# A hybrid decoder layer on one core: another order of the down products, and other instruction orders at four places

## The chip, the cores and the metric

The kernel runs as one program on one core of a Trainium2 chip. The metric is the device time of the whole program in microseconds, as the median of several runs; lower is better. Before the change three runs took 2069.5, 2070.79 and 2072.06 us.

The engines are written as in the profile: PE (TensorE) multiplies, DVE (VectorE), ACT (ScalarE) and POOL (GpSimd) work on elements, SP (SyncE) issues DMAs. Each works off its own list of instructions in order; they meet only through semaphores.

## The reference

One decoder layer on x of 1024 tokens by 1024 features, in float32:

```
h = RMSNorm(x)
[q,k,v,g | x_rnn,gate_rnn | m_ret,m_rnn] = h @ W_in             # 1024 x 10240
y_ret = (silu(g) * HeadNorm(Retention(rot(q), rot(k), v))) @ W_ret_o    # 4 heads, chunks of 128
y_rnn = (RG_LRU(CausalDWConv4(x_rnn)) * gelu(gate_rnn)) @ W_rnn_o
x = x + (sigmoid(m_ret) * y_ret + sigmoid(m_rnn) * y_rnn) @ W_out
up = CausalDWConv3(RMSNorm(x) @ W_up)                           # 1024 x 5632
x = x + (silu(up[:, :2816]) * up[:, 2816:]) @ W_down            # 2816 x 1024
out = RMSNorm(x)
```

## The kernel before, in words

Every product of two float32 matrices is made of three matmuls (`mm3`, lines 308 to 310): each operand is split into a high part (ACT rounds it to fp32r, "hi") and a rest (DVE subtracts, "lo"), and hi hi, hi lo and lo hi are added in PSUM. So in front of nearly every matmul stand one ACT and one DVE instruction.

Three sections use Winograd's form of Strassen's scheme, in which seven products of half-size blocks replace eight. The input projection (28 blocks of 256 columns) and the FFN's up projection (22 blocks) have the weights W split as B11 to B22, of which DVE makes T1 to T4 (`combine_t13`, `combine_t2`, `combine_t4`), and the activations as A11 to A22, S1 to S4. A block runs the products q = 0 to 6: B11 A11 (P1), B21 A12, T4 A22, T2 S2, T1 S1, T3 S3, B22 S4, twelve matmuls of 128x512 each. Some accumulate on an earlier result: ACT first copies P1, U1, P5, U2 out of PSUM (`in_copy`, `copy_u`, lines 1313 and 1593), and the products q = 3, 5, 6 wait for copies. `prep_hi` (L1279) and `prep_lo` (L1842) split weights. DVE adds the quarters (`in_c`, L1947; `add_c11` and so on, L2319 to L2328) and, in the FFN, runs the convolution's taps (L2339), with ACT's `conv_first` and `silu_gate` (L1638, L1645). Blocks 0 and 1 are written out, their products interleaved by `ORDER01` in the FFN; the rest runs in loops (`steady`).

During the input projection DVE also prepares the down weights: in each of blocks 0 to 21 SP loads four tiles (`load_tq`), DVE combines them (`combine_down`, L1952 to L1956), POOL stores them to `scr_t`.

Retention runs head by head in eight steps j. PE does the scores, turns k and the last output, makes the outputs (`outs`), the state's update, and from step 5 on the product with W_ret_o (`reto`). DVE scales and masks the scores (L2132), splits ktm and scores (L2138, L2141), makes the statistics of the head norm (L2074 to L2097) and updates the state (L2160). POOL splits v and the state (`lo_parts`, L833; `state_lo`, L839), in head 0 as in the others.

The down product has seven products p of five chunks each (35 chunks i; two k-tiles a chunk, three in the fifth, on four token tiles), in the order t4, b11, b21, t2, t1, t3, b22. SP loads the FFN's output h from DRAM (`down_h`) into `hq`, after POOL has stored it there (L871), and ACT and DVE split weights (L1699, L2403) and h (L1721, L2410) chunk by chunk; two chunks are in flight, since a chunk's ACT splits wait until PE has finished the chunk two before (`d_b`). The first product, t4, takes h22, whose last rows are those of the FFN's last group. DVE makes sums of h (`s1` to `s4`, L2424), adds results to x (`add_down`, L2452) and at the end, behind the split of chunk 34, normalises: ACT squares and sums a token tile and takes the root (`square`, L1739, L1742), DVE takes the reciprocal and scales (`finish`, L2458, L2461), SP stores. Tiles 4 to 7 come first; tiles 0 to 3 take the last product's results (L2517).

All orders are written out by hand in the code; there is no scheduler.

## Time and profile before

| | |
|---|---|
| median of three runs | 2070.79 us |
| the profiled execution | 2074.71 us |
| its span | 2073.0 us |
| PE busy | 2010.2 us, 97% |
| DVE, ACT, POOL busy | 1404.2, 903.5, 249.1 us |
| mean granted TensorE clock | 0.992 |

The span is the time from the first to the last instruction of the profiled execution; its own time is 1.7 us longer. Engine L12 means line 12 of the kernel. In a timeline each row is one instruction, or several alike: start, duration, engine, line, operation, what it writes and reads, count, and in brackets how long the engine had been idle before it and on whom it waited. Matmuls are pipelined: the duration is longer than the distance from one start to the next. DMA moves 137 GB/s on average. The clock is given as a share of 2.4 GHz.

### The profile page before, as it was taken

The page shows a single profiled execution, that of the slowest core. Times are in us where ns is not written, and L with a number is a line of the kernel's source. Part 1 is how long each engine was busy: PE and PEld are TensorE (multiplying, and loading weights), DVE is VectorE, ACT ScalarE, POOL GpSimd, SP SyncE. Part 2 cuts the span into 40 slices and gives each one's busy share as a digit, 9 for nine tenths or more (in the row PEclk, how much of TensorE's full clock was granted, in tenths as well). Part 3 has the DMA queues.
Part 4 walks back from the last instruction along what each step waited for, and adds up shares of the span by engine and source line. Part 5 has one row for each costly group of instructions (what it writes and reads, how often), then busy time and mean ns, then how long its engine had stood idle before and what let it go on. Part 6 is the DMA issues. An engine that isn't in the chain of part 4 may idle for free.

```text
span 2073.0 us, 26838 instructions
## 1 busy us (share of the span) xinstructions
PE 2010.2 (97%) x10100; PEld 1706.6 (82%) x10100; DVE 1404.2 (68%) x1707; ACT 903.5 (44%) x1154; POOL 249.1 (12%) x194
## 2 busy tenths in 40 slices
PE   7999999999999999998899999999999999999998
PEld 6788888888889999887688887898788888887886
DVE  6887876776544444513877877847888788774866
ACT  6343353343445555402444443345544544543334
POOL 0000000000000000012454545200000000000000
PEclk9999999999999999999999999999999999999999
DMA  5245544444444342345233234741222122247533
GB/s 208 102 152 182 177 157 172 162 169 148 159 146 159 133 153 102 142 161 174 80 123 116 83 116 130 258 140 59 84 81 101 61 81 101 70 157 244 188 101 127
DMA packets 188697, 283.10 MB, mean 137 GB/s; under 512 B 9808, under 2 KB 132048, under 8 KB 188368
## 3 DMA queue, kind: packets, MB, share of 16 engines
q1 hardware_dynamic: 168320, 204.52, 29.9%
q0 software_dynamic: 20304, 77.60, 9.4%
q8 instruction: 46, 0.75, 0.1%
q14 instruction: 27, 0.22, 0.0%
HBM read 198.20 MB, written 83.89 MB: 136 GB/s over the span
## 4 chain that ended last, share of the span: by engine, by line
PE 82%; DVE 9%; issue 4%; ACT 2%; DMA 1%; POOL 1%; SPq 0%; DVEq 0%; ACTq 0%; POOLq 0%
PE ps L308 27%; PE ps L310 27%; PE ps L309 27%; DVE wx L1842 1%; POOL msg L859 1%; PE ps L1056 1%; DMA raw<-w_ret_o 1%; DVE ost L1790 1%; DVE xb L2461 0%; DVE stage L1947 0%; PE ps L369 0%; DVE hsd L2410 0%; DVE tt L1804 0%; DVE ws L291 0%; PE ps L1087 0%
## 5 line engine op out<-in xcount | busy, mean ns | idle before, releaser
L1279 ACT ACTIVATE wx<-raw 128x1024 fp32r<-128x1024 f32 (+1 forms) x152 | 137.4, 906 | 284.1 <-DVE raw L1818 157.7
L308 PE MATMUL ps<-xs,wx 128*128 128x512 f32 x612 | 239.4, 391 | 5.4 <-ACT ub L1593 3.2
L310 PE MATMUL ps<-xs,wx 128*128 128x512 f32 x612 | 238.9, 390 | 0.0
L309 PE MATMUL ps<-xs,wx 128*128 128x512 f32 x612 | 238.8, 390 | 0.0
L291 DVE TENSOR_TENSOR ws<-raw,ws 128x2048 fp32r<-128x2048 f32 x32 | 74.4, 2324 | 180.6 <-ACT ws L287 180.6
L308 PE MATMUL ps<-sc,wx 128*128 128x512 f32 x448 | 175.6, 392 | 4.6 <-ACT ub L1313 4.6
L1842 DVE TENSOR_TENSOR wx<-raw,wx 128x1024 fp32r<-128x1024 f32 (+1 forms) x152 | 156.2, 1028 | 34.6 <-ACT wx L1279 34.6
L310 PE MATMUL ps<-sc,wx 128*128 128x512 f32 x448 | 175.0, 391 | 0.0
L309 PE MATMUL ps<-sc,wx 128*128 128x512 f32 x448 | 174.9, 390 | 0.0
L309 PE MATMUL ps<-ws,actv 128*128 128x256 f32 x512 | 144.9, 283 | 0.0
L310 PE MATMUL ps<-ws,actv 128*128 128x256 f32 x512 | 144.9, 283 | 0.0
L308 PE MATMUL ps<-ws,actv 128*128 128x256 f32 x512 | 144.9, 283 | 0.0
L308 PEld LDWEIGHTS ps<-xs,wx 128*128 128x128 f32 x612 | 115.3, 188 | 31.9 <-ACT ub L1593 3.6
L309 PEld LDWEIGHTS ps<-xs,wx 128*128 128x128 f32 x612 | 115.3, 188 | 23.9
L310 PEld LDWEIGHTS ps<-xs,wx 128*128 128x128 f32 x612 | 115.2, 188 | 23.9
L308 PE MATMUL ps<-actv,wx 128*128 128x512 f32 x336 | 130.7, 389 | 0.0
L309 PE MATMUL ps<-actv,wx 128*128 128x512 f32 x336 | 130.7, 389 | 0.0
L310 PE MATMUL ps<-actv,wx 128*128 128x512 f32 x336 | 130.7, 389 | 0.0
L1313 ACT ACTIVATE ub<-ps 128x512 f32<-128x512 f32 x112 | 66.3, 596 | 143.4 <-PE ps L310 140.8
L308 PE MATMUL ps<-wsd,hsd 128*128 128x512 f32 x308 | 121.4, 394 | 4.1 <-DVE hsd L2410 3.0
L309 PE MATMUL ps<-wsd,hsd 128*128 128x512 f32 x308 | 121.0, 393 | 0.0
L310 PE MATMUL ps<-wsd,hsd 128*128 128x512 f32 x308 | 120.9, 392 | 0.0
(266 smaller groups left out, 4954.5 us busy)
## 6 DMA issues: line engine op xcount, KB each, us to landing
raw<-w_in SPq DMA_DIRECT2D x80, 512.0 KB, 5.2
scr<-ost POOLq DMA_DIRECT2D x32, 1024.0 KB, 5.2
raw<-w_up SPq DMA_DIRECT2D x44, 512.0 KB, 3.9
tq<-w_down SPq DMA_DIRECT2D x88, 128.0 KB, 2.4
scr_t<-tq POOLq DMA_DIRECT2D x22, 512.0 KB, 3.2
scr_h<-vt POOLq DMA_DIRECT2D x11, 1024.0 KB, 4.3
scr_v<-ost POOLq DMA_DIRECT2D x8, 1024.0 KB, 4.6
qkv<-scr SPq DMA_DIRECT2D x64, 128.0 KB, 3.0
```

The costliest lines, as they stand in the source:

```text
L291: dve.tensor_tensor(ws[:, slot, LO, 0:n], raw[:, slot, 0:n], ws[:, slot, HI, 0:n].bitcast(F32), ALU.subtract).then_inc(w_split[slot], 1)
L308: pe.matmul(out, w(HI), x(HI), start=first, stop=False, skip_group_check=True)
L309: pe.matmul(out, w(HI), x(LO), start=False, stop=False, skip_group_check=True)
L310: return pe.matmul(out, w(LO), x(HI), start=False, stop=last, skip_group_check=True)
L859: pool.tensor_tensor(msg[:, n % 4, :], msg[:, n % 4, :], yacc[:, t, half * HALF:(half + 1) * HALF], ALU.mult).then_inc(sem["mx_mul"], 1)
L1056: last = pe.transpose(ps[:, 5, m * P:(m + 1) * P], on[:, slot, m * P:(m + 1) * P], ident[:, :])
L1279: act.activation(dst, src, ACT.Copy).then_inc(sem["f_hi"], 1)
L1313: act.activation(ub[:, which, :], ps[:, 4 * u + BANKS[q], :], ACT.Copy).then_inc(sem["f_u"], 1)
L1790: ins = dve.scalar_tensor_tensor(out=dst, in0=s_, scalar=w, in1=dst, op0=ALU.mult, op1=ALU.add)
L1842: dve.tensor_tensor(dst, src, hi.bitcast(F32), ALU.subtract).then_inc(sem["f_lo"], 1)
```

## The change

1. Down: the order of products becomes b11, t4, t2, t1, t3, b22, b21, so that the first takes h11; h22, h21 and h12 are loaded in another order, the sums of h are made in other chunks, results are added in other chunks, and `down_h_lo(0)` stands ahead of two adds of the last FFN block.
2. End: the squares and scalings of tiles 4 to 7 go into chunks 30 to 34; tiles 0 to 3 end with the left half.
3. Input projection: in block 0 ACT copies P1 before it prepares S4 and B22, and U1 before T4 of block 1; DVE makes one sum earlier. The down weights are prepared in blocks 0, 2, 4, 6 and 8 to 25, and A21 is read back at block 28 instead of 25.
4. Head 0: DVE splits the state instead of POOL.
5. FFN: T1 and T3 of block 0, t4 and b1 of blocks 1 and 2 are split elsewhere in the order, blocks 2 and 3 are written out, and block 2 copies P1 before the convolution.

The diff, cut to its core:

```diff
@@ -36,12 +36,13 @@
...
 D_CHUNKS = 7 * len(D_TILES)
-D_W = ["t4", "b11", "b21", "t2", "t1", "t3", "b22"]
+D_W = ["b11", "t4", "t2", "t1", "t3", "b22", "b21"]
 D_BANK = [0, 4, 0, 4, 0, 4, 0]
-D_FIRST = [True, True, True, False, True, False, False]
-D_LAST = [True, False, True, False, False, True, True]
+D_FIRST = [True, True, False, True, False, False, True]
+D_LAST = [False, True, False, False, True, True, True]
 D_ORDER = [4, 5, 6, 7, 0, 1, 2, 3]
 W_TILES = 2 * KD
+W_AT = [0, 2, 4, 6] + list(range(8, 26))
...
@@ -496,7 +497,12 @@
...
-    S3_DONE, S2_DONE, S1_DONE, S4_DONE = 0, 5, 10, 15
+    H_ORDER = [("s3", 0), ("s3", 1), ("s3", 2), ("s2", 0), ("s3", 3), ("s2", 1), ("s3", 4), ("s2", 2), ("s2", 3), ("s2", 4)]
+    H_ORDER += [(n, c) for n in ("s1", "s4") for c in range(5)]
+    def summed(name, c):
+        return H_ORDER.index((name, c)) + 1
...
                         sp_.dma_start(dst[:, :], a[src]).then_inc(sem["cs_in"], 16)
-                if b == LAST_QK + 3:
+                if b == IN_BLOCKS:
...
@@ -729,48 +735,47 @@
...
             sp_.wait_ge(sem["f_pr"], produced(BLOCKS - 1, 2) + W_P)
-            down_h(0, 1, 1, 0, 2, "h22a")
-            down_h(0, 1, 1, 2, 4, "h22b")
+            down_h(0, 0, 0, 0, 2, "h11a")
+            down_h(0, 0, 0, 2, 4, "h11b")
             sp_.wait_ge(sem["f_pr"], produced(BLOCKS - 1, 4) + W_P)
-            down_h(0, 1, 1, 4, 9, "h22c")
+            down_h(0, 0, 0, 4, 11, "h11c")
             down_w(2)
             sp_.wait_ge(sem["f_pr"], produced(BLOCKS - 1, 6) + W_P)
-            down_h(1, 0, 0, 0, 3, "h11a")
+            down_h(1, 1, 1, 0, 3, "h22a")
             down_w(3)
-            down_h(1, 0, 0, 3, 5, "h11b")
+            down_h(1, 1, 1, 3, 6, "h22b")
...
-            down_h(1, 0, 0, 5, 8, "h11c")
+            down_h(1, 1, 1, 9, 11, "h22d")
             down_w(6)
-            down_h(1, 0, 0, 8, 11, "h11d")
-            down_w(7)
             sp_.wait_ge(sem["x1_st"], 32)
...
             sp_.wait_ge(sem["x1_st3"], 16)
-            down_x(1, 0, "x_bk0")
+            down_x(0, 0, "x_bk0")
+            down_w(7)
+            down_h(2, 1, 0, 0, 4, "h21a")
             down_w(8)
-            down_h(2, 0, 1, 0, 4, "h12a")
+            down_h(2, 1, 0, 4, 8, "h21b")
             down_w(9)
...
@@ -843,8 +848,6 @@
...
                     store_rnno(3)
-                if j:
-                    state_lo(0, j - 1)
             with pool.Fori(1, HEADS) as h:
...
@@ -1202,8 +1205,10 @@
...
                     pe.wait_ge(sem["f_c"], 4 * BLOCKS + W_C)
-                elif p >= 2 and t % 2 == 0:
+                elif 2 <= p < 6 and t % 2 == 0:
                     pe.wait_ge(sem["d_add"], 2 * (p - 2) + t // 2 + 1)
+                elif p == 6 and t % 2 == 0:
+                    pe.wait_ge(sem["d_add"], 11 + t // 2)
...
@@ -1296,13 +1301,11 @@
...
             prep_hi(0, 0, "t2")
-            comb_hi(sc1[:, HI, :, :], cbf, 8)
+            comb_hi(sc1[:, HI, :, :], cbf, 7)
             evac_job(FIRST_PAIR, 1, 2, ACT.Sigmoid, 0)
...
             prep_hi(0, 0, "t13")
-            comb_hi(sc4[:, LO, :, :], caf, 11)
-            prep_hi(0, 0, "b22")
...
@@ -1331,6 +1334,9 @@
...
+            in_copy(0, 0, U_P1)
+            comb_hi(sc4[:, LO, :, :], caf, 11)
+            prep_hi(0, 0, "b22")
             for b in range(IN_BLOCKS):
...
@@ -1338,16 +1344,19 @@
...
                     in_out(b - 1)
-                in_copy(b, u, U_P1)
+                    in_copy(b, u, U_P1)
                 if more:
...
                     prep_hi(b + 1, 1 - u, "b1")
+                    if b == 0:
+                        in_copy(b, u, U_U1)
                     act.wait_ge(sem["f_t4"], b + 2)
...
                     prep_hi(b + 1, 1 - u, "t4")
-                in_copy(b, u, U_U1)
+                if b:
+                    in_copy(b, u, U_U1)
                 if not more:
...
@@ -1599,6 +1608,8 @@
...
             for k in range(4):
+                if k == 2:
+                    prep_hi(0, 0, "t13")
                 turned(12 + k + 1)
...
@@ -1606,7 +1617,6 @@
...
             s_hi(S2, a22f, lambda c: act.wait_ge(sem["s2_f"], c + 1))
-            prep_hi(0, 0, "t13")
             s_hi(S1, s1f, lambda c: act.wait_ge(sem["s1_f"], c + 1))
...
@@ -1662,28 +1672,38 @@
...
             next_b1_hi(1, 1)
+            copy_u(1, 1, U_U2)
             next_t4_hi(1, 1)
-            silu_gate(0)
-            copy_u(1, 1, U_U2)
             next_t13_hi(1, 1)
...
             def steady(b, u, more=True):
+                second = isinstance(b, int) and b == 2
                 act.wait_ge(sem["f_t2"], b + 1 + W_T)
...
                 prep_hi(b, u, "t2b22")
+                if second:
+                    copy_u(b, u, U_P1)
                 conv_first(b - 1, 1 - u)
-                copy_u(b, u, U_P1)
-                if more:
+                if not second:
+                    copy_u(b, u, U_P1)
+                if second:
                     next_b1_hi(b, u)
+                    copy_u(b, u, U_U1)
+                    copy_u(b, u, U_P5)
                     next_t4_hi(b, u)
+                    silu_gate(0)
                 else:
-                    down_w_hi(0)
-                copy_u(b, u, U_U1)
-                copy_u(b, u, U_P5)
-                if not more:
-                    down_h_hi(0)
-                if u:
-                    silu_gate(b - 1)
+                    if more:
+                        next_b1_hi(b, u)
+                        next_t4_hi(b, u)
+                    else:
+                        down_w_hi(0)
+                    copy_u(b, u, U_U1)
+                    copy_u(b, u, U_P5)
+                    if not more:
+                        down_h_hi(0)
+                    if u:
+                        silu_gate(b - 1)
                 copy_u(b, u, U_U2)
...
@@ -1699,28 +1719,30 @@
...
-            H_LOADS = [(("h22a",), ("h22b",), ("h22c",), ("h22c",), ("h22c", "h22d")),
-                       (("h11a",), ("h11a", "h11b"), ("h11b", "h11c"), ("h11c",), ("h11d",)),
-                       (("h12a",), ("h12a",), ("h12b",), ("h12b",), ("h12c",))]
-            H_SUMS = {3: (0, S2_DONE), 4: (1, S1_DONE), 5: (3, S3_DONE), 6: (2, S4_DONE)}
+            H_LOADS = {0: (("h11a",), ("h11b",), ("h11c",), ("h11c",), ("h11c",)),
+                       1: (("h22a",), ("h22a", "h22b"), ("h22b",), ("h22c",), ("h22c", "h22d")),
+                       6: (("h12a",), ("h12a",), ("h12b",), ("h12b",), ("h12c",))}
+            H_SUMS = {2: (1, "s2"), 3: (0, "s1"), 4: (2, "s3"), 5: (1, "s4")}
...
+                if p in H_LOADS:
+                    q = (0, 1, None, None, None, None, 3)[p]
                     for name in H_LOADS[p][c]:
...
                     q, done = H_SUMS[p]
-                    act.wait_ge(*late_count("d_s", done + c + 1))
+                    act.wait_ge(*late_count("d_s", summed(done, c)))
...
-            with act.Fori(1, GROUPS - 1) as g:
+            for u in range(2):
+                steady(2 + u, u)
+            with act.Fori(2, GROUPS - 1) as g:
                 for u in range(2):
...
@@ -1745,9 +1767,8 @@
...
                 down_h_hi(i)
-                if i >= D_CHUNKS - 2:
-                    for n in range(2):
-                        square(2 * (i - D_CHUNKS + 2) + n)
+                if i in (30, 31, 32, 33):
+                    square(i - 30)
             for n in range(4, KT):
...
@@ -1902,10 +1923,10 @@
...
             comb(c2f, cbf, c3f, ALU.subtract)
+            step_done(6)
+            comb(cbf, c2f, caf, ALU.add)
+            comb_lo(sc2[:, LO, :, :], c2f, sc2[:, HI, :, :], 2)
             prep_lo(0, 0, "b1", 1)
-            step_done(6)
-            comb_lo(sc2[:, LO, :, :], c2f, sc2[:, HI, :, :], 2)
-            comb(cbf, c2f, caf, ALU.add)
             combine_t4(0, 0, 0, 1)
...
@@ -2169,6 +2192,12 @@
...
                     accumulate(*n)
+            def state_lo(h, j):
+                slot = j % 2
+                dve.wait_ge(sem["s_hi"], h * 7 + (j + 1))
+                dve.tensor_tensor(sts[:, slot, LO, :, :], stt[:, :, :], sts[:, slot, HI, :, :].bitcast(F32),
+                                  ALU.subtract).then_inc(sem["s_sp"], 1)
...
@@ -2293,20 +2322,20 @@
...
             combine_t4(1, 1)
+            prep_lo(0, 0, "t13")
             s_lo(A22, a22f, 0, 5)
             s_lo(A22, a22f, 1, 6)
+            prep_lo(1, 1, "t4")
             for c in range(2):
...
                 dve.tensor_tensor(a22f[:, k, :], a22f[:, k, :], s3f[:, k, :], ALU.subtract).then_inc(sem["s2_f"], 1)
-            prep_lo(1, 1, "t4")
             for c in range(2):
...
                 s_lo(S2, a22f, c, 7 + c)
-            prep_lo(0, 0, "t13")
             s_lo(S1, s1f, 0, 9)
...
@@ -2381,11 +2410,11 @@
...
             def ending(b, u, more=True):
+                if not more:
+                    down_h_lo(0)
                 add_c22_c21(b, u)
...
                     prep_lo(b + 1, 1 - u, "t13")
-                else:
-                    down_h_lo(0)
                 add_c12(b, u)
...
-            body(1, 1)
-            ending(1, 1)
-            with dve.Fori(1, GROUPS - 1) as g:
+            combine_t13(2, 0)
+            combine_t2(2, 0)
+            prep_lo(2, 0, "b1")
+            combine_t4(2, 0)
+            conv_tap(0, 0, 0, 1)
+            add_c11(1, 1)
+            prep_lo(2, 0, "t4")
+            add_c22_c21(1, 1)
+            conv_tap(0, 0, 0, 2)
+            prep_lo(2, 0, "t13")
+            add_c12(1, 1)
+            prep_lo(2, 0, "t2b22")
+            conv_tap(0, 0, 1, 1)
+            conv_tap(0, 0, 1, 2)
+            body(2, 0)
+            multiply(0)
+            ending(2, 0)
+            steady(1, 1)
+            with dve.Fori(2, GROUPS - 1) as g:
                 for u in range(2):
...
                 if i == 6:
-                    add_down(0, 1, 0, "x_bk0")
+                    add_down(0, 0, 0, "x_bk0")
+                elif i == 7:
+                    s3(0)
+                elif i == 8:
+                    s3(1)
+                elif i == 9:
+                    s3(2)
+                    s2(0)
+                elif i == 10:
+                    s3(3)
+                    s2(1)
                 elif i == 11:
-                    add_down(1, 0, 0, "x_bk1")
+                    s3(4)
+                    s2(2)
                 elif i == 12:
-                    s3(0)
-                    s3(1)
+                    s2(3)
+                    add_down(1, 1, 0, "x_bk1")
                 elif i == 13:
-                    s3(2)
-                    s3(3)
+                    s2(4)
                 elif i == 14:
-                    s3(4)
-                    s2(0)
+                    s1(0)
...
+                    add_down(3, 1, 1, "x_bk3")
+                elif i in (22, 23, 24, 25):
+                    s4(i - 22)
                 elif i == 26:
+                    add_down(4, 1, 0, "x_bk1")
+                elif i == 27:
+                    s4(4)
+                elif i == 28:
                     add_down(4, 1, 1, "x_bk3")
-                elif i in (27, 28, 29):
-                    s4(i - 25)
                 elif i == 31:
-                    add_down(5, 1, 0, "x_bk0")
-                elif i == 32:
-                    add_down(5, 1, 1, "x_bk3")
-            dve.wait_ge(*late_count("g_in", 16))
-            for n in range(4):
-                finish(n)
+                    add_down(5, 0, 1, "x_bk2")
+                    dve.wait_ge(*late_count("g_in", 16))
+                    finish(0)
+                elif i in (32, 33, 34):
+                    finish(i - 31)
+            def add_last(t):
+                dve.wait_ge(sem["d_ps"], t + 1)
+                dve.tensor_tensor(xb[0][:, t, 0:HALF], xb[0][:, t, 0:HALF], ps[:, t, :], ALU.add).then_inc(sem["d_add"], 1)
             for t in range(4):
-                dve.wait_ge(sem["d_ps"], t + 1)
-                dve.tensor_tensor(xb[0][:, t, HALF:], xb[0][:, t, HALF:], ps[:, t, :], ALU.add).then_inc(sem["d_add"], 1)
+                add_last(t)
...
```

## Rows read from the trace of the kernel before

**Rows 1.** The page, part 1: busy time, share of the span, instructions.
```profile
PE 2010.2 (97%) x10100; PEld 1706.6 (82%) x10100; DVE 1404.2 (68%) x1707; ACT 903.5 (44%) x1154; POOL 249.1 (12%) x194
```

**Rows 2.** Waits of PE over the span: waiter, releaser, total, times, longest.
```profile
PE ps L308 <- DVE qkvs L2085: 5.3, 4, 2.1
PE ps L308 <- ACT ub L1313: 4.6, 6, 1.8
PE ps L308 <- ACT ub L1593: 3.2, 1, 3.2
PE ps L308 <- DVE hsd L2410: 3.0, 2, 2.8
```

**Rows 3.** Windows: length, busy of PE, PEld, DVE, ACT, POOL, clock, DMA share, GB/s.
```profile
67.00:93.00 26.00, 22.42 (x91) 17.79 (x91) 19.33 (x19) 12.18 (x16) 0.72 (x1) 0.93 0.29 102
...
955.00:1015.00 60.00, 45.45 (x196) 35.25 (x194) 42.06 (x69) 24.65 (x44) 24.95 (x14) 0.89 0.46 141
...
1460.00:1485.00 25.00, 21.54 (x87) 17.31 (x88) 22.93 (x25) 13.75 (x17) 0.72 (x1) 0.93 0.13 43
1485.00:1600.00 115.00, 115.00 (x509) 95.24 (x508) 92.96 (x95) 55.95 (x68) 2.16 (x3) 1.00 0.25 91
...
1872.00:1880.00 8.00, 7.61 (x21) 6.01 (x22) 2.52 (x3) 0.75 (x1) 0.00 (x0) 0.59 0.90 323
```

**Rows 4.** Timeline of PE, input projection, block 0.
```profile
77.79 0.47 PE L308 MATMUL ps<-sc,wx 128*128 128x512 f32 x1 [1.74 <-ACT ub L1313]
...
85.31 0.50 PE L308 MATMUL ps<-sc,wx 128*128 128x512 f32 x1 [1.84 <-ACT ub L1313]
```

**Rows 5.** Timeline of ACT, input projection, block 0.
```profile
77.07 0.58 ACT L1313 ACTIVATE ub<-ps 128x512 f32<-128x512 f32 x1
```

**Rows 6.** Timeline of DVE, retention, head 0.
```profile
994.71 1.98 DVE L2141 TENSOR_TENSOR scs<-sc,scs 128x128 fp32r<-128x128 f32 x1
...
1034.56 0.28 DVE L2141 TENSOR_TENSOR scs<-sc,scs 128x128 fp32r<-128x128 f32 x1
```

**Rows 7.** Timeline of POOL, retention, head 0.
```profile
990.14 1.50 POOL L833 TENSOR_TENSOR qkvs<-qkv,qkvs 128x512 fp32r<-128x512 f32 x1 [3.05 <-ACT qkvs L1457]
994.14 2.40 POOL L839 TENSOR_TENSOR state_s<-state,state_s 128x1024 fp32r<-128x1024 f32 x1 [2.50 <-ACT state_s L1504]
```

**Rows 8.** Timeline of PE, FFN, blocks 0 to 2.
```profile
1439.77 0.47 PE L308 MATMUL ps<-xs,wx 128*128 128x512 f32 x1 [0.71 <-DVE xs L2238]
...
1460.29 0.49 PE L308 MATMUL ps<-xs,wx 128*128 128x512 f32 x1 [0.88 <-DVE wx L1842]
...
1471.93 0.50 PE L308 MATMUL ps<-xs,wx 128*128 128x512 f32 x1 [3.17 <-ACT ub L1593]
```

**Rows 9.** Timelines of DVE and of ACT, FFN, blocks 0 to 2.
```profile
1437.28 1.22 DVE L1842 TENSOR_TENSOR wx<-tt,wx 128x1024 fp32r<-128x1024 f32 x1
...
1471.30 0.58 ACT L1593 ACTIVATE ub<-ps 128x512 f32<-128x512 f32 x1
```

**Rows 10.** Timeline of PE, first chunks of the down product.
```profile
1847.54 0.47 PE L308 MATMUL ps<-wsd,hsd 128*128 128x512 f32 x1 [1.08 <-issue]
...
1872.39 0.77 PE L308 MATMUL ps<-wsd,hsd 128*128 128x512 f32 x1 [2.81 <-DVE hsd L2410]
```

**Rows 11.** Timelines of DVE and of ACT, first chunks of the down product.
```profile
1846.22 1.22 DVE L2410 TENSOR_TENSOR hsd<-hq,hsd 128x1024 fp32r<-128x1024 f32 x1
...
1868.97 1.49 ACT L1721 ACTIVATE hsd<-hq 128x1536 fp32r<-128x1536 f32 x1 [3.25 <-DMA hq<-scr_h]
```

**Rows 12.** Timelines of PE and of DVE, the end.
```profile
2063.38 0.39 PE L310 MATMUL ps<-wsd,hsd 128*128 128x512 f32 x1
...
2055.33 1.28 DVE L2461 SCALAR_TENSOR_TENSOR xb<-xb,rms_rs,gbc 128x1024 f32<-128x1024 f32 x1
...
2066.33 0.68 DVE L2517 TENSOR_TENSOR xb<-xb,ps 128x512 f32<-128x512 f32 x1
...
2068.75 1.28 DVE L2461 SCALAR_TENSOR_TENSOR xb<-xb,rms_rs,gbc 128x1024 f32<-128x1024 f32 x1
```

More of the change, by code:

```diff
@@ L554, in _ @@
                                   ).then_inc(sem["a21_st"], 16)
-                if 1 <= b <= W_TILES:
-                    load_tq(b - 1)
+                if b - 1 in W_AT:
+                    load_tq(W_AT.index(b - 1))
                 if b == LAST_XR + 3:
@@ L751, in _ @@
             sp_.wait_ge(sem["x1_st3"], 16)
-            down_x(1, 0, "x_bk0")
+            down_x(0, 0, "x_bk0")
+            down_w(7)
+            down_h(2, 1, 0, 0, 4, "h21a")
             down_w(8)
-            down_h(2, 0, 1, 0, 4, "h12a")
+            down_h(2, 1, 0, 4, 8, "h21b")
             down_w(9)
-            down_h(2, 0, 1, 4, 8, "h12b")
+            down_h(2, 1, 0, 8, 11, "h21c")
             down_w(10)
-            down_h(2, 0, 1, 8, 11, "h12c")
             down_w(11)
-            down_x(0, 0, "x_bk1")
+            down_x(1, 0, "x_bk1")
             down_w(12)
-            down_h(3, 1, 0, 0, 4, "h21a")
             down_w(13)
-            down_h(3, 1, 0, 4, 8, "h21b")
+            down_x(0, 1, "x_bk2")
             down_w(14)
-            down_h(3, 1, 0, 8, 11, "h21c")
             down_w(15)
-            down_x(0, 1, "x_bk2")
+            down_x(1, 1, "x_bk3")
             down_w(16)
+            sp_.dma_start(gbc[:, :], a["final_g"]).then_inc(late_sem("g_in"), 16)
             down_w(17)
-            down_x(1, 1, "x_bk3")
+            down_h(3, 0, 1, 0, 4, "h12a")
             down_w(18)
-            sp_.dma_start(gbc[:, :], a["final_g"]).then_inc(late_sem("g_in"), 16)
+            down_h(3, 0, 1, 4, 8, "h12b")
+            down_h(3, 0, 1, 8, 11, "h12c")
             for i in range(19, D_CHUNKS):
@@ L803, in _ @@
             for b in range(IN_BLOCKS):
-                if b < W_TILES:
-                    store_tq(b)
+                if b in W_AT:
+                    store_tq(W_AT.index(b))
                 store(*in_pair(b), rows(IN_COL[b]))
@@ L906, in in_product @@
                     if early and b == 0:
-                        pe.wait_ge(sem["q_st"], 7)
+                        pe.wait_ge(sem["q_st"], 8)
                     pe.wait_ge(sem["f_lo"], in_prepared(b, "t2"))
@@ L1735, in square @@
                 t = D_ORDER[n]
-                act.wait_ge(sem["d_add"], 14 if n < 4 else 14 + n - 3)
+                act.wait_ge(sem["d_add"], 12 if n < 4 else 14 + n - 3)
                 if n >= 2:
@@ L1987, in _ @@
                 in_c(b, u, 3)
-                if b < W_TILES:
-                    combine_down(b)
+                if b in W_AT:
+                    combine_down(W_AT.index(b))
             a_p = prm[:, PRM["a_param"]:PRM["a_param"] + 8]
@@ L2142, in step @@
                                   ALU.subtract).then_inc(sem["sc_sp"], 1)
+                if first and j:
+                    state_lo(0, j - 1)
                 if j in (1, 5) and not (first and j == 1):
@@ L2346, in multiply @@
                 dve.tensor_tensor(vt[:, :, :], vt[:, :, :], gt[:, :, :], ALU.mult).then_inc(sem["a_mul"], 1)
+            s_lo(S1, s1f, 1, 10)
             add_c11(0, 0)
-            s_lo(S1, s1f, 1, 10)
             prep_lo(1, 1, "t2")
@@ L2407, in down_h_lo @@
                 p, c, k0, n = down_at(i)
-                u, q = i % 2, (0, 1, 2, 0, 1, 3, 2)[p]
+                u, q = i % 2, (0, 1, 1, 0, 2, 1, 3)[p]
                 dve.wait_ge(sem["dh_hi"], i + 1)
@@ L2428, in s3 @@
                 dve.wait_ge(*late_count(("h21a", "h21a", "h21b", "h21b", "h21c")[c], 16))
-                sum_h(3, 1, 3, ALU.subtract, c)
+                sum_h(2, 0, 2, ALU.subtract, c)
             def s2(c):
-                dve.wait_ge(*late_count("d_s", S3_DONE + c + 1))
-                sum_h(0, 0, 3, ALU.subtract, c)
+                dve.wait_ge(*late_count("d_s", summed("s3", c)))
+                sum_h(1, 1, 2, ALU.subtract, c)
             def s1(c):
-                dve.wait_ge(*late_count("d_s", S2_DONE + c + 1))
-                sum_h(1, 0, 1, ALU.add, c)
+                dve.wait_ge(*late_count("d_s", summed("s2", c)))
+                sum_h(0, 1, 0, ALU.add, c)
             def s4(c):
-                sum_h(2, 2, 0, ALU.subtract, c)
+                dve.wait_ge(*late_count(("h12a", "h12a", "h12b", "h12b", "h12c")[c], 16))
+                sum_h(1, 3, 1, ALU.subtract, c)
             def add_down(p, half, n, loaded):
```

24 lines of the change are left out of this document (7 added, 17 removed).

## The prediction

> **What bounds the kernel now.** I read the page first: PE is busy 2010.2 of 2073.0 us, 97% [rows 1]. So time can only come from three places: gaps between matmuls, matmuls issued at the lower TensorE clock, and the stretch behind the last one. The table of waits for PE gives the gaps. Of those it lists, the largest that the edits can reach are four: activations of the input projection (4.6 us, 6 times), the split of q and k in retention (5.3, 4 times), one copy of the FFN (3.2, once) and one split of the down product (2.8 of 3.0) [rows 2]. The windows show what the first table hides. At full clock 509 matmuls fill 115 us, 0.227 us each, so a product of twelve takes 2.72; in stretches with a gap the granted clock falls to a mean of 0.93, 0.89, 0.93 and 0.59 [rows 3]. The engine is then at 1.2 GHz instead of 2.4 for a while, and the stretch times (1 - clock) is lost beside the gap: 26 x 0.07 = 1.8 us, 25 x 0.07 = 1.75, 8 x 0.41 = 3.3 [rows 3]. Each fall followed waits, so who removes the wait gets both.
>
> **Input projection.** The product T2 S2 of block 0 waits 1.74 us for the copy of P1, T3 S3 then 1.84 us for the copy of U1 [rows 4]. The P1 copy ran at 77.07 [rows 5] although its product had ended near 70.5 (77.79 less the wait of 1.74 and its restart of 0.15 is 75.9, and two more products had run by then): ACT did `comb_hi(sc4)` and the B22 split first, and the former waited for DVE. The edit puts the copy ahead of both; ACT is then free at about 69.5 and copies at 70.7. U1 no longer stands behind `prep_hi(1, "t4")`, so it follows its product at once. What is late next is DVE's split of sc1, the eleventh count of q_st: DVE gets 2.2 us earlier into `comb(cbf, ...)`, which fills its wait for ACT, and I place the split's end at 72, the need at 78.6. T4's split and the P5 copy are at 82.5, the need at 84.05. So both waits go: 1.74 + 1.84, two restarts of 0.15 and the 1.8 us of low clock, 5.7 in all. The other four waits of that row of the table (4.6 - 3.58 = 1.0 us [rows 2]) stay: they fall in blocks 1, 3, 5 and 7, behind the `combine_down` of blocks 0, 2, 4 and 6, and `W_AT` keeps exactly those. The down tiles taken from the odd blocks move to blocks 22 to 25, where DVE does them as it does in 8 to 21: nothing, at most 1 us. A21 is loaded some 50 us later and has some 35 us before the V product asks for it: nothing. POOL and SP only lose waits here.
>
> **Head 0.** DVE is the engine that sets the step of some 8.6 to 9.2 us. Its split of the scores, 128x128, takes 1.98 us there and 0.28 us where POOL is idle [rows 6]; POOL's split of the state began 0.57 us before and ran 2.40 [rows 7]. The edit takes the state's split to DVE, right behind that instruction. It is 128x1024 with two SBUF operands; the row of that shape has 1.22 us [rows 9], 1.14 issue to issue. Per step DVE saves 1.70 and adds 1.14: 0.55 us. Steps 1 to 5 can show it; in 6 and 7 reto products keep PE filled. In two of the five (j = 2 and 4) DVE's next instruction waits for PE, which runs at the low clock there, so the split only fills a wait. Three times 0.55, and a little of the 60 x 0.11 = 6.6 us of low clock [rows 3]: I take 2.0. Bounds: -1 (the addition shows in steps 6 and 7), +5 (clock stays up in steps 2 and 4).
> A rule speaks against this edit. The Trainium skill, "SBUF — State Buffer", section "Who interferes with whom", says that a VectorE instruction with two SBUF inputs and a GpSimd instruction that reads SBUF exclude each other for a whole instruction. The slow split of the scores agrees; by the rule the moved split, too, could be held by POOL's remaining split of V.
> In the trace V's split lies from 990.14 to 991.64 and the moved one would start at about 994.9 [rows 6, 7], 3 us clear, so I price this at nothing; if they met, each meeting would hold DVE for up to 1.50 us.
>
> **FFN, blocks 0 to 3.** PE waits 0.71 at 1439.77 for the split of S1, 0.88 at 1460.29 for b1 of block 2, 3.17 at 1471.93 for the P1 copy of block 2 [rows 8]. (1) The T1/T3 split goes from 1437.28 (1.22 us, [rows 9]) into DVE's idle time before A22, and ACT's part likewise. S2 still ends at the same time, since `t4` only changes places with it, so the 1.12 us saved on t4x come back as two waits in (0,3); the S1 split is then ready at 1438.5 and T1 S1 starts at 1438.77: 1.0 us, and 0.2 of restart. (2) b1's split of block 2 stands ahead of a tap and an add. ACT's conv_first and b1 follow PE, so DVE ends it at 1457.9 with PE there at about 1458.0: 1.0 us. (3) P1 of block 2 is copied before conv_first instead of behind it; before it started at 1471.30 [rows 9], now at about 1461.5, needed at 1466.2. The wait of 3.17 + 0.15 and the 1.75 us of low clock go: 5.0. Late next: DVE's t2b22 split at 1466.4 (0.2 us late) and, in block 3, the P1 copy behind conv_first, whose second half waits for add_c12: 0.2 late. DVE carries more before block 3 and reaches its t2b22 4.9 us later in the block than before, but it is busy 93.0 of 115 us [rows 3], 3.6 us free in each block of 19.05: caught up by block 4. Sum 7.2 - 0.4 = 6.8; bounds 3.5 and 7.5.
>
> **Down.** (1) Chunk 0 starts at 1847.54, put down to "issue" with 1.08 us; DVE's split of h ends at 1846.22 + 1.22 = 1847.44 [rows 10, 11], so it is that. It stood behind two adds that wait for the last U2 copy; moved ahead of them it ends near 1843.9: 1.2 us. If instead the loop's exit is the cause, nothing. (2) Chunk 4 waits 2.81 us for a split [rows 10], because ACT's part began at 1868.97 [rows 11], when the last FFN group, stored and read back, had landed. B11 A11 reads no row of that group, and the load h22d is now wanted by chunk 9, some 27 us later. The wait with its restart, 2.96, and 3.0 of the 3.3 us of low clock: 6.0. Next late in chunk 4 is DVE's split after the ACT one, level with PE to 0.1 us, as in chunk 9 before. (3) Sums of h: two of 1.14 us beside 2.3 us of splits in a chunk of 5.44; s2(0) is ready 1.8 us into chunk 9, ACT asks at 1.0, PE 8.2 us in. All seven products pass DVE in time by my count: nothing; a late h21b would be 3 us and its clock.
>
> **The end.** `finish(0)` to `finish(3)` keep DVE from 2055.14, just ahead of the first scaling [rows 12], for four times 1.4 us, to 2060.7, when tile 0 had been ready since 2057.6 (the last matmul's end, 2063.77, less three tiles of nine matmuls). Now they lie beside matmuls, and ACT's squares are spread over four chunks (the table load of 1.3 us included they fit in 5.44), which also gives back the 0.2 + 0.15 us wait at 2055.37. The last add started at 2066.33 [rows 12]; it can start at 2063.85, behind the last matmul (2063.38 + 0.39 [rows 12]). The chain behind it, 2068.75 - 2066.33 = 2.42 to the last scaling [rows 12], is the same: 2.5 + 0.4 = 2.9.
>
> **Sum.** 5.7 + 2.0 + 6.8 + 1.2 + 6.0 + 2.9 = 24.6 us off. The profiled execution took 2074.71 us around a span of 2073.0: it would take 2050.1. It is 3.9 above the median of the three runs, 2070.79, and the edits are the same in both: 2046.2.
>
> **Rivals.** (A) A part comes back: in the FFN DVE, 4.9 us behind, makes PE wait 1 us more in blocks 2 and 3 and the clock falls (1.75), and head 0 gives nothing (2.0): 4.8 us, 2051, somewhere from 2049 to 2054. For it: four margins under 0.3 us in my placing. Against: the waits of 0.71 and 0.88 [rows 8] were followed by full clock. (B) The clock stays up in head 0 and its steps shorten fully: 3 us more, 2043. For: 6.6 us of low clock lie there [rows 3]; against: PE still waits 1.5 us a step. (C) The other side: DVE never recovers its 4.9 us in the FFN loop. With DVE over 19.05 us of work a block, PE would wait in each of the 18 blocks left; from 1.4 us a block on the gain is gone, and at 2 us with clock it is 2046.2 + 36 = 2082. Against it: 3.6 us free a block [rows 3]. (D) The reorderings ahead of the down products do nothing, because other waits stand right behind those removed; only down and tail count: 10.1 us, 2060.7. Against: the next needs placed above, all within 0.4 us. (E) The state's split meets POOL's split of V in head 0: 1.50 us [rows 7] in each of five steps, 7.5, so 2053.7. Against: the 3 us between them. That is what the rule of the page "SBUF — State Buffer" in the Trainium skill would bring.
>
> **Numbers.** Forecast 0.65, own range 2044 to 2048.5; A 0.20; B 0.07; D 0.03; E 0.03; C 0.02. The range 2042.5 to 2052 takes in A and B. Anything past 0.2% (4.1 us, what a measurement here can tell) is faster in all but C: faster 0.97, same 0.01, slower 0.02.
>
> **What would show it.** Right: no PE wait between 70 and 95, L1313 down to four short ones; score splits at 0.28 us in head 0; FFN block 3 starting 6.8 us nearer to block 0; no half-rate matmuls at the start of down; last matmul's end to the end of the span 9.2 before, 6.8 after. Wrong: a wait on DVE's wx in FFN blocks 2 to 4, on hsd in chunks 4 or 10, or on POOL in head 0.

## The result

The changed kernel takes 2048.66 us (median of 4 runs, 2047.09 to 2051.48) against 2070.94 (4 runs): a ratio of 0.9895, interval 0.9883 to 0.9907, so 22.3 us faster. Run once more beside seven runs of before it took 2048.0 (2047.72 to 2048.47) against 2071.23, 0.9886 [0.987, 0.9903], 23.2 us. Forecast were 2046.2 and 24.6 us off, with a range of 2044 to 2048.5 for the forecast alone and of 2042.5 to 2052 in all: 2048.66 lies just outside the first, 2048.0 inside it.

The profiled executions differ by more: 2074.71 against 2047.54, 27.2 us. That gap between a pair of profiles and a pair of medians is the main lesson below.

### The profile page after: what moved, and what is told of

It reads as the page before. It is cut to its first block, busy times and chain, and to the rows that moved or that the text cites. A ratio compares the mean times of both kernels' runs of the same rounds, so it can differ in the third digit from the quotient of the medians.

```text
span 2045.9 us, 26772 instructions
## 1 busy us (share of the span) xinstructions
PE 1999.9 (98%) x10100; PEld 1700.8 (83%) x10100; DVE 1407.6 (69%) x1714; ACT 904.0 (44%) x1154; POOL 232.8 (11%) x187
## 4 chain that ended last, share of the span: by engine, by line
PE 89%; DVE 7%; issue 1%; ACT 1%; DMA 1%; SPq 0%; DVEq 0%; ACTq 0%
PE ps L309 29%; PE ps L311 29%; PE ps L310 29%; DVE wx L1863 1%; PE ps L1059 1%; DVE ost L1811 1%; DMA raw<-w_ret_o 0%; PE ps L370 0%; DVE stage L1968 0%; DVE tt L1825 0%; PE ps L1090 0%; PE ps L1012 0%; DMA raw<-w_in 0%; DVE gt L2368 0%; DVE vt L2368 0%
```

## The profile after

The page's first part (PEld is the loading of PE's weights), and PE's table of waits (waiter, releaser, total, times, longest):

```profile
PE 1999.9 (98%) x10100; PEld 1700.8 (83%) x10100; DVE 1407.6 (69%) x1714; ACT 904.0 (44%) x1154; POOL 232.8 (11%) x187
```

```profile
PE ps L309 <- DVE ktm L2159: 6.9, 9, 1.6
PE ps L309 <- DVE qkvs L2106: 4.3, 4, 1.5
PE ps L309 <- DVE mix L2219: 1.7, 1, 1.7
PE ps L309 <- DVE xs L2267: 1.6, 3, 0.6
PE ps L309 <- ACT ub L1316: 1.2, 4, 0.3
PE ps L309 <- ACT ub L1602: 0.4, 1, 0.4
```

Against [rows 2]: the copies of the input projection are down to four waits of 0.3, the FFN's copy from 3.2 to 0.4, and no wait on hsd is left. PE is busy 10.3 us less than before [rows 1] for the same 10100 matmuls, and the mean granted clock is 0.998 instead of 0.992: fewer of them ran at 1.2 GHz. The windows that answer to [rows 3] (length, PE, PEld, DVE, ACT, POOL, clock, DMA share, GB/s) say where:

```profile
67.00:93.00 26.00, 26.00 (x116) 21.52 (x115) 22.09 (x25) 11.77 (x16) 1.51 (x2) 1.00 0.35 118
955.00:1010.00 55.00, 41.58 (x192) 32.39 (x191) 43.58 (x83) 26.63 (x48) 14.30 (x10) 0.94 0.42 128
1450.00:1475.00 25.00, 24.90 (x110) 20.00 (x108) 24.68 (x26) 14.80 (x18) 0.72 (x1) 1.00 0.23 85
1826.00:1860.00 34.00, 34.00 (x152) 28.05 (x151) 22.64 (x19) 15.51 (x16) 0.72 (x1) 1.00 0.86 315
```

In the input projection the P1 copy, at 77.07 before [rows 5], now runs at 71.09 (timeline of ACT), ahead of sc4:

```profile
71.09 0.60 ACT L1316 ACTIVATE ub<-ps 128x512 f32<-128x512 f32 x1 [0.94 <-PE ps L311]
72.47 1.92 ACT L1289 ACTIVATE sc<-caf 128x2048 fp32r<-128x2048 f32 x1 [0.78 <-DVE sc L1909]
```

Head 0, timeline of DVE: the split of the scores takes 0.28 us instead of 1.98 [rows 6], with the moved split of the state behind it.

```profile
986.45 0.28 DVE L2162 TENSOR_TENSOR scs<-sc,scs 128x128 fp32r<-128x128 f32 x1
986.65 1.22 DVE L2199 TENSOR_TENSOR state_s<-state,state_s 128x1024 fp32r<-128x1024 f32 x1
```

FFN, timeline of ACT: P1 of block 2 at 1450.19, then conv_first; the SiLU's table load only at 1464.16.

```profile
1450.19 0.58 ACT L1602 ACTIVATE ub<-ps 128x512 f32<-128x512 f32 x1
1451.35 1.25 ACT L1648 ACTIVATE vt<-fst,prm 128x1024 f32<-128x1024 f32 x1 [0.58 <-DVE fst L2353]
...
1464.16 1.28 ACT L1655 ACT_TABLE_LOAD   x1
```

The down product, timelines of DVE and of PE: the split for chunk 0 ends at 1826.9, before the adds (fst), and PE starts without a wait. At the end the last add (2039.15) follows the last matmul (2038.73) by 0.42 us, where 2.95 lay between them before [rows 12].

```profile
1825.67 1.23 DVE L2439 TENSOR_TENSOR hsd<-hq,hsd 128x1024 fp32r<-128x1024 f32 x1 [4.20 <-ACT hsd L1741]
1828.04 0.69 DVE L2352 TENSOR_TENSOR fst<-ub 128x512 f32<-128x512 f32 x1 [1.15 <-ACT ub L1602]
...
2039.15 0.69 DVE L2569 TENSOR_TENSOR xb<-xb,ps 128x512 f32<-128x512 f32 x1
2041.58 1.28 DVE L2507 SCALAR_TENSOR_TENSOR xb<-xb,rms_rs,gbc 128x1024 f32<-128x1024 f32 x1
```

```profile
1829.33 0.39 PE L309 MATMUL ps<-wsd,hsd 128*128 128x512 f32 x1
...
2038.73 0.39 PE L311 MATMUL ps<-wsd,hsd 128*128 128x512 f32 x1
```

## Experiments: the four parts, each alone

Each kernel is the one before with one part of the diff. The other schedule of the down weights (`W_AT`) and the later reading back of A21 are in none of the four.

```
only_in    ACT: in_copy(P1) ahead of comb_hi(sc4); in_copy(U1) ahead of prep_hi(1, "t4")
           DVE: comb(cbf, c2f, caf) ahead of comb_lo(sc2)
only_h0    - pool: if j: state_lo(0, j - 1)      + dve: if first and j: state_lo(0, j - 1)
only_ffn   PREP, t13/t4/S1 splits, b1, adds, U2 ahead of silu_gate(0), P1, blocks 2 and 3 written out
only_down  D_W, D_FIRST, D_LAST, loads, sums, down_h_lo(0) ahead of the adds, squares and finish
```

> The kernel before with the input projection's part of the change alone: on ScalarE the copy of P1 ahead of the split of sc4 and of B22, the copy of U1 ahead of the split of T4; on VectorE cbf before the split of sc2. The schedule of the down tiles (W_AT) and everything behind stay as before. Theory: 5.7 us off, from the waits of 1.74 and 1.84 us, two restarts of 0.15 and 1.8 us of low clock; T2 S2 of block 1 starts 5.1 to 5.7 us nearer to the first matmul. Rival: in the profile of the whole change 1.9 us more than forecast is gone in head 0 and 1.2 at its end, and part of that could be carried over from here (later stages start earlier against loads): then this alone gives 6 to 8. Second rival: loads by time, not by matmul, hold the stages behind, and less than 4 arrives at the end.

> The kernel before with the state's split of head 0 on VectorE instead of GpSimd, nothing else. Theory as forecast: 2.0 us off (three steps of 0.55 and a little clock). Rival from the two traces: from the first scores to the first reto product 3.95 us went, and the step ends show the clock up in step 0; if that comes from the split, this alone gives 3.5 to 4.5 us. If the extra comes from the shorter wait at the first scores (1.39 us before, 0.91 after), it gives 2 to 2.8 and the granted clock between the scores' start and 1015 stays near 0.89.

> The kernel before with the FFN part alone: the T1/T3 split ahead of A22, t4 of block 1 ahead of the forming of S2, S1's second split ahead of the first add, b1 of block 2 ahead of a tap and an add, P1 of block 2 copied ahead of conv_first, blocks 2 and 3 written out ahead of the loop. Theory: 6.3 to 6.8 us off, most of it the wait of 3.17 with the clock behind it (5.0). Rival: the W_out section's 1.18 us wait belongs to this part's other placing and goes too: 7.5 to 8. Second rival: the code written out ahead of the loop costs loading, less than 5 arrives.

> The kernel before with the down products' part alone: B11 A11 first and A22 later, the sums of h and their loads in the new order, the split of h for chunk 0 ahead of two adds, tiles 0 to 3 scaled beside the last five chunks. Theory: 1.2 (chunk 0) + 6.0 (chunk 4 and its clock) + 2.9 (the end) = 10.1 us off. Rival: the clock falls in another chunk in part of the executions (the kernel after showed 2047.1 to 2051.5 us), so the median gives 7 to 8. Second rival: chunk 0's wait is the loop's exit, 8.9.

Measured against 20 runs of before (2071.33): only_in 2066.0, ratio 0.9974 [0.9963, 0.9985], 5.3 us off; only_h0 2068.3, 0.9990 [0.9981, 0.9999], 3.0; only_ffn 2064.21, 0.9967 [0.9955, 0.9979], 7.1; only_down 2063.53, 0.9962 [0.9949, 0.9975], 7.8. The sum, 23.2, is the whole change, as well as medians can tell: the interval of each part is about 2 us to either side. The section lengths below are finer. Head 0 apart, the sections that a part edits have the same length in that part alone as in the whole change (input projection 535.6 in both, FFN 426.4 in both, down 209.5 and 209.4), so the parts do not help or hinder each other there, and `W_AT`, which only the whole has, costs nothing in the input projection. The down part gave 2.3 us less than the 10.1 forecast.

The runs of before lie between 2066.99 and 2074.82, and these kernels also say a good part of why. Each holds, in three of its four places, the code of before once more. I took the start of each stage's first and last matmul from PE's timeline; the differences are section lengths, free of what happens elsewhere. "As before" are all profiled executions with that section's old code (p1_alone and silu_alone of the next group too), "as after" those with the new, from all groups; best4 is left out of head 0, which it edits, the three best kernels out of the input projection, and tail_late out of the last row.

| section | before | others as before | mean | as after |
|---|---|---|---|---|
| input projection | 541.13 | 541.37, 539.78, 541.17, 539.74, 541.24 | 540.74 | 535.55 to 535.63 |
| first scores to first reto product (head 0) | 46.04 | 44.80, 45.43, 46.12, 44.86, 46.16 | 45.57 | 42.10 to 44.92, mean 43.77 |
| FFN | 432.60 | 432.65, 432.61, 432.70 | 432.64 | 426.33 to 426.38 |
| FFN's last matmul to the first of down | 1.47 | 1.47 in all | 1.47 | 0.22 |
| down, first to last matmul start | 215.84 | 214.46, 213.18, 214.71, 213.27, 213.06 | 214.09 | 209.40 to 209.52 |
| last matmul start to end of span | 9.6 | 9.6 to 9.7 | 9.6 | 7.1 to 7.2 |

By the means: 5.1 + 1.8 + 6.3 + 1.2 + 4.7 + 2.5 = 21.6, beside the 22.3 and 23.2 of the medians. In the profile of before the down section is 1.75 longer than the mean, the input 0.4, head 0 0.5: 2.6 of its excess of 3.9 us sit in the places that the change edits.

What differs is the clock. In head 0 the windows 962:1022 of all traces have one of three values, and the lengths of the section go with them: with the old code 46.04, 46.12, 46.16 and 45.43 at a clock of 0.89, and 44.80 and 44.86 at 0.91; with the new code 44.92 and 44.91 at 0.89, 43.60, 43.61, 43.61 and 43.63 at 0.91, and 42.10 at 0.94. At the same clock the edit is worth 1.1 to 1.2 us (0.5 against the one of 45.43); the rest of the 1.8 comes from less time at 1.2 GHz in the executions of the new code. Whether the edit brings that or chance, seven executions against six cannot tell. The windows of before, only_h0 and after:

```profile
962.00:1022.00 60.00, 45.45 (x201) 35.50 (x200) 48.02 (x79) 29.00 (x50) 26.26 (x16) 0.89 0.36 106
962.00:1022.00 60.00, 46.77 (x208) 36.49 (x206) 48.16 (x88) 29.22 (x52) 14.29 (x10) 0.89 0.35 103
962.00:1022.00 60.00, 45.52 (x214) 35.51 (x213) 51.09 (x99) 28.41 (x52) 12.95 (x11) 0.94 0.36 105
```

In the down product the clock differs behind the same wait. Chunk 4, PE's timeline and then the window of 8 us from about where the wait ends (clock in the third column from the right), in only_in:

```profile
1865.40 0.77 PE L308 MATMUL ps<-wsd,hsd 128*128 128x512 f32 x1 [2.67 <-DVE hsd L2414]
```

```profile
1865.00:1873.00 8.00, 7.60 (x27) 6.17 (x28) 2.52 (x3) 1.01 (x2) 0.00 (x0) 0.79 0.93 331
```

and in only_h0:

```profile
1868.77 0.47 PE L308 MATMUL ps<-wsd,hsd 128*128 128x512 f32 x1 [2.94 <-DVE hsd L2416]
```

```profile
1868.00:1876.00 8.00, 7.23 (x32) 6.00 (x33) 2.90 (x3) 1.09 (x2) 0.00 (x0) 1.00 0.92 319
```

Before had 2.81 and 0.59 [rows 3, 10]. Of these three the longest wait was followed by 2.4 GHz (matmuls every 0.23 us), the others by a time at 1.2 GHz. Over six executions of this wait (2.67 to 2.96 us) the window's clock was 0.59, 0.79, 0.79, 1.00, 1.00 and 1.00. In the input projection it fell in four of six (0.93 or 1.00 over 67:93). In the FFN it fell in all four executions that have the wait of 3.17 to 3.19 us for the P1 copy (0.93 over 25 us each).

## Experiments: which step of the FFN part carries it

```
p1_late     (changed kernel)  - if second: copy_u(b, u, U_P1)     conv_first first again
p1_alone    (kernel before)   + in block 2: copy_u(b, u, U_P1) ahead of conv_first(b - 1, 1 - u)
silu_alone  (kernel before)   - silu_gate(0) ahead of copy_u(1, 1, U_U2)
                              + silu_gate(0) behind copy_u(b, u, U_P5) of block 2
```

In the last two ACT's blocks 2 and 3 are written out ahead of the loop as well, since block 2 needs an order of its own.

> The changed kernel with one step undone: in block 2 of the FFN, P1 is copied behind conv_first again. Theory: the copy is late by 3.2 us, PE waits 3.2 to 3.3 and loses 1.4 at the low clock behind it: 4.6 us slower than the changed kernel. With the clock sized as in the prediction 5.0. Rival: conv_first now has its input earlier, since DVE's second half of block 1 stands before the copy; the wait is under 2 us, no clock falls, 1 to 2 us slower.

> The kernel before with one step of the FFN part alone: in block 2 P1 is copied ahead of conv_first. The prediction gave this step 5.0 us; undoing it in the changed kernel cost nothing in the FFN section (its trace has a wait of 0.54 us there). Theory now: what holds the copy is ScalarE's queue ahead of it, the SiLU of block 0 (1461.64 to 1466.27 in the trace of before) and the splits behind it; conv_first adds only 2.6 us. So alone it takes 2.6 us off the wait of 3.17 and with luck the 1.4 us of clock: FFN section 2.6 to 4.0 shorter. Rival (as predicted): 4.7 to 5.0 shorter, wait gone.

> The kernel before with another step of the FFN part alone: the SiLU of block 0, with its table load, stands behind the U1 and P5 copies of block 2 instead of ahead of the U2 copy of block 1; P1 stays behind conv_first. Theory: U2's copy of block 1 runs some 4.5 us earlier, VectorE's adds of block 1 follow it, conv_first does not wait for them, and the P1 copy is in time to 0.5 us: the wait of 3.17 and its clock go, FFN section 4 to 4.7 us shorter. Rival: conv_first's second half waits for the last add of block 1, which VectorE reaches no earlier, under 1.5 us.

The FFN section measures 426.36 in p1_late (the changed kernel: 426.33 and 426.38), 431.49 in p1_alone and 429.85 in silu_alone (before: 432.64). So putting P1 ahead of conv_first is worth 1.1 us alone and nothing in company; moving the SiLU is worth 2.8 alone; all of the part 6.3. Each is less than was expected: 4.6 us slower for p1_late, 2.6 to 4.0 shorter for p1_alone, 4 to 4.7 shorter for silu_alone. The steps (1) and (2) of the prediction had no run of their own; by PE's waits they gave 1.8 us (0.47, 1.12, 0.17, 0.71 and 0.88 before, 0.47, 0.57 and 0.55 after). By the medians p1_late is 1.7 us slower than the changed kernel beside it (2049.66 against 2048.0, intervals of the ratios overlapping; nothing in its FFN accounts for that; head 0, which it does not edit, is 1.3 longer in its trace), p1_alone 0.9992 [0.9982, 1.0001], silu_alone 0.9989 [0.9979, 0.9998].

In p1_alone the wait of 3.17 became one of 2.44 and a new one of 0.91 at 1475.40, so no waiting was saved; the granted clock over 1460:1485 is 1.00 instead of 0.93, and the 1.1 us come from that.

Why P1 alone fails is in the timelines. Those of before already have the next late instruction, DVE's split of T2 and B22. It ended at 1471.04, 0.26 us ahead of the start of the P1 copy, and it stands behind adds that waited for the U2 copy, which ACT made right behind the SiLU:

```profile
1465.30 1.06 ACT L1645 ACTIVATE gt<-gt 128x1024 f32<-128x1024 f32 x1 [1.30 <-DVE gt L2339]
1466.27 0.58 ACT L1593 ACTIVATE ub<-ps 128x512 f32<-128x512 f32 x1
```

```profile
1466.88 0.69 DVE L2323 TENSOR_TENSOR fst<-ub 128x512 f32<-128x512 f32 x1 [1.61 <-ACT ub L1593]
...
1469.82 1.22 DVE L1842 TENSOR_TENSOR wx<-raw,wx 128x1024 fp32r<-128x1024 f32 x1
```

p1_alone leaves all that as it was. ACT: the SiLU still stands ahead of the U2 copy (1463.83); P1 follows at 1466.21, early enough.

```profile
1459.20 1.28 ACT L1645 ACT_TABLE_LOAD   x1
...
1463.83 0.58 ACT L1593 ACTIVATE ub<-ps 128x512 f32<-128x512 f32 x1
...
1466.21 0.58 ACT L1593 ACTIVATE ub<-ps 128x512 f32<-128x512 f32 x1
```

DVE: its adds wait for that U2 copy, and the split of T2 and B22 stands behind the adds, to 1468.6.

```profile
1464.44 0.69 DVE L2329 TENSOR_TENSOR fst<-ub 128x512 f32<-128x512 f32 x1 [1.61 <-ACT ub L1593]
...
1467.39 1.22 DVE L1848 TENSOR_TENSOR wx<-raw,wx 128x1024 fp32r<-128x1024 f32 x1
```

PE waits for it, in the same place:

```profile
1468.74 0.49 PE L308 MATMUL ps<-xs,wx 128*128 128x512 f32 x1 [2.44 <-DVE wx L1848]
```

With the SiLU moved alone U2 is copied at 1461.2, but DVE is in its taps until 1464.9 and PE still waits 1.28 us, for P1. DVE's split ends at 1469.03 there, and PE starts at 1469.71; an estimate from these two is that P1 in time as well would still leave a wait of some 0.7 us for the split, so DVE's order has to change too. No run has both of ACT's moves with DVE's old order, so this is not shown. With all moves made, P1's own place is worth 0.54 us of wait that is made good later in the section (p1_late):

```profile
1459.88 0.50 PE L309 MATMUL ps<-xs,wx 128*128 128x512 f32 x1 [0.54 <-ACT ub L1602]
```

## Experiments: the changed kernel again, and its end

```
after_again  no edit
tail_late    - elif i == 31: finish(0)   elif i in (32, 33, 34): finish(i - 31)
             + for n in range(4): finish(n)      behind the last chunk's splits
```

> The changed kernel itself once more, for a median over more runs and a second trace. Theory: the four parts alone gave 5.3, 3.0, 7.1 and 7.8 us, 23.2 in sum, and the first runs 22.3, so 22 to 24 here; the pair of traces showed 27.2 only because the profiled execution of before was 3.9 us above its median. Rival: the parts help each other and the pair of traces is right, 25 to 27.

> The changed kernel with the scaling of tiles 0 to 3 put back behind the last chunk's splits; the squares stay spread over chunks 30 to 33. Theory: the four scalings keep VectorE until 2.5 us after it could start the last adds: 2.5 us slower, last matmul's end to the end of the span 9.2 instead of 6.8. Rival: with std and squares early the four run back to back as soon as the last split ends, some 5 us before the last matmul's end, and cost 0.5 us or nothing.

after_again: above. Its profiled execution took 2047.99, 0.45 us from the first, though head 0 is 1.5 longer in it and the stretch from reto to the FFN 0.6 shorter. tail_late: 2051.73, 3.7 us above it; its trace runs 9.65 us from the last matmul's start to the end, against 7.17, so 2.5 us as expected, where the rival had 0.5 or nothing. The profiled execution, 2052.57, is 4.6 above after_again's; of the other 2.1, 1.75 lie between head 0's first product with W_ret_o and the FFN, where it has a wait of 1.54 on ws that after_again lacks, and 0.4 ahead of the first scores. The last of the four scalings ends where the adds begin; the last add starts at 2044.18, 2.93 us behind the last matmul:

```profile
2037.36 1.29 DVE L2507 SCALAR_TENSOR_TENSOR xb<-xb,rms_rs,gbc 128x1024 f32<-128x1024 f32 x1
2038.56 1.28 DVE L2569 TENSOR_TENSOR xb<-xb,ps 128x512 f32<-128x512 f32 x2
```

## Experiments: the waits that are left

```
best1  ACT: if b in (0, 1, 3, 5, 7): in_copy(b, u, U_U1) ahead of the t4 split
       DVE: heads 1 to 3, step 3: both accumulates ahead of split_lo; mixed_lo(7) ahead of accumulate
best3  the ACT edit of best1; DVE: split_lo(out_block(0)) at t == 5, mixed_lo(7) ahead of accumulate
       SP: load_columns(out_block(2)) at n == 12
best4  best3; head 0, j in (2, 4, 6): qk_lo(0, j + 1) ahead of stats
```

> The changed kernel with three further orders: (1) in blocks 1, 3, 5 and 7 of the input projection the copy of U1 ahead of the split of T4, for the four waits of 0.30 us (0.45 each with the restart, 1.8); (2) in step 3 of heads 1 to 3 both accumulates ahead of the split of the weight, for three waits of 0.55 (0.7 each, 2.1); (3) at the end of retention the split of the eighth mixed tile ahead of an accumulate and an add, for 1.2 of the wait of 1.69. Theory: 5.1 us faster than the changed kernel. Rival: the waits are only moved, less than 1.5.

> The changed kernel with (1) in blocks 1, 3, 5 and 7 of the input projection the copy of U1 ahead of the split of T4 (2.4 us in the trace of the version before this one), (2) at the end of retention the weight's split one accumulate later and the eighth mixed split ahead of an accumulate, for the 1.8 us that PE waits there, (3) the load of W_out's third block issued behind the thirteenth pair of loads instead of the sixteenth, for the wait on ws of 0 to 2 us that differs from one execution to the next. Theory: 2.4 + 1.3 + 0.9 (the mean over the traces) = 4.6 us faster than the changed kernel, 2043.4, and the runs lie closer together. Rival: the earlier load holds back the pairs behind it and the wait turns up on mix at the fifth block: 2 us, 2046.

> The same as best3 and in steps 2, 4 and 6 of head 0 the split of q and k ahead of the statistics, into VectorE's idle time of 0.45 to 0.64 us. Theory: 0.45 in each of two or three steps, 1 us faster than best3, first reto product 1 us nearer to the first scores. Rival: the statistics, now 0.1 to 0.2 us later, hold the normalisation, for which PE waits 1.4 us a step as well: same or 0.5 us slower.

best1: 2046.93, 1.1 us below the changed kernel beside it, not 5.1. The four copies' waits went: the input projection is 533.1 long in all three traces instead of 535.6, 2.5 us. The order in step 3 made its waits longer, 0.87 instead of 0.55, because the second accumulate waits for PE. The wait on mix went and one of 1.97 on ws came; but such a wait on ws comes and goes where nothing near it was edited (1.18 in before, none in both traces of the changed kernel, 1.32 in p1_late), so it cannot be put down to the edit. best3: 2046.3 (0.9885 [0.9868, 0.9901] to before), best4: 2046.8 (0.9888 [0.9872, 0.9905]); the changed kernel had 0.9886 in its second set, so none of the three is shown to be faster, and only the 2.5 us of the input projection are seen in the traces. Expected were 4.6 us for best3 and 1 more for best4. In best3 the load came early and the wait on ws stayed (PE's timeline):

```profile
1328.25 0.39 PE L309 MATMUL ps<-ws,mix 128*128 128x256 f32 x1 [1.37 <-DVE ws L292]
```

ACT began that weight's split at 1323.90, right behind its last mix split and without a wait for the load, which SP had issued at 1306.04: it stands behind all sixteen mix splits, not behind a DMA. In best4 head 0 is 43.14 at a clock of 0.94 against best3's 43.63 at 0.91; the only other trace at 0.94 has 42.10, so nothing speaks for that edit.

## Why the prediction held, and where it did not

**Input projection** (5.7): right. Both waits went, the next needs were met, the four others stayed at 0.30, the moved down tiles cost nothing. It measured 5.1 over the executions, 5.6 from those in which the clock had fallen and 4.2 from the two in which it had not.

**Head 0** (2.0): right in mechanism, 1.8 by the sections, 3.0 [0.2, 3.9] by the median. At equal clock it is 1.1 to 1.2, less than the three times 0.55, and whether the edit or chance brought the rest by the clock is open, so part of the agreement may be luck. Against the pair of profiles, 3.9, the forecast looked too small: that came from one short execution after (42.10, at a clock of 0.94). The state's split did not meet POOL's split of V, as placed; rival E fell.

**FFN** (6.8): the size was right, 6.3, the attribution not. Step (3), "P1 of block 2 is copied before conv_first instead of behind it ... 5.0", failed. I read the releaser of the wait, the P1 copy, and took the instruction that had just stood before it for the cause. The SiLU ahead of the U2 copy of block 1 was the start, worth 2.8 us by itself where P1's place was worth 1.1: copy, DVE's adds, conv_first's second half and T2's split all hang on it. The diff moved it, and the prediction did not price that. The "late next", DVE's split at 0.2 us, holds only with every other move made; with P1 alone it is 2.44 us late.

**Down, chunk 0** (1.2): 1.2, and it was the split and not the loop's exit. **Chunk 4** (6.0): the mechanism was right, no wait is left there, but by the section's mean 4.7 was to be had, and 0.4 of that is the wait of 0.22 at 2055.37 with its restart, which the prediction counts under the end. That leaves 4.3. The mis-sized term is "3.0 of the 3.3 us of low clock": (1 - 0.59) x 8 was one execution's fall; over the six of old code the lost time is 3.3, 1.7, 1.7 and three times nothing, 1.1 on average. **The end** (2.9): 2.5 behind the last matmul and the 0.4 at 2055.37, as forecast.

**The step from the profile to the median** failed too, "It is 3.9 above the median of the three runs ... and the edits are the same in both". The excess lay partly in the edited places, so it could not be gained in the median. The two clock terms are most of the 3.0 us between 24.6 and the sections' 21.6: 1.9 for chunk 4 (3.0 - 1.1) and 0.6 for the input projection (1.8, in four of six). That 22.3 came out by the medians is within their intervals.

Rivals A, C and D named other mechanisms, and none is seen: behind blocks 2 and 3 there is one new wait, of 0.37 us at 1481.04 for the P1 copy of block 3 (placed at 0.2), no loss a block in the loop, and none of the parts is without effect. B's full clock in head 0 did not come (0.94).

## What to carry to other kernels

Where a profiled execution lies above the median, find the stretch that holds the excess before pricing an edit: executions of kernels that share the stretch give its spread for nothing, and section lengths from matmul to matmul resolve 0.1 us where medians resolve 2, as long as the clock does not fall differently in them; where it does, compare executions of equal granted clock. Price low clock behind a wait as a mean over executions, not from one window. For a wait, follow the releaser's own queue back until something stands there that need not: the instruction next to the late one is often late for the same reason.
